# Attention by key with stacked hi and lo operands, and one output product for all mixer blocks

## What is computed

```python
x = x + 0.5 * _swiglu(_rmsnorm(x, g_f1), w_g1, w_u1, w_d1)
h = _rmsnorm(x, g_mix)
u, c_gate, b_gate, q, k, v, f_logit, q_mem = jnp.split(h @ w_in, bounds, axis=-1)
y_conv = b_gate * conv                  # conv over c_gate * u, 3 taps, 256 channels
q = _head_rms(q, gq_fox); k = _head_rms(k, gk_fox)            # 8 heads of 64
cum = jnp.cumsum(jnp.concatenate([past_logf, logf], axis=1), axis=1)
# forgetting attention ("fox"), causal; a decode row sees 128 past keys and its own 32
s = q . k * scale + cum_q - cum_k;  y_fox = softmax(s) @ v
# memory attention, 4 heads, 256 memory keys for the prompt, 256 cached ones for decode
y_mem = softmax(q_mem . mk * scale) @ mv
x = x + concat(y_conv, y_fox, y_mem) @ w_out
x = x + 0.5 * _swiglu(_rmsnorm(x, g_f2), w_g2, w_u2, w_d2);  x = _rmsnorm(x, g_fin)
```

## Time and profile before

| | |
|---|---|
| runs | 2314.63 us median of 3 (2314.17 to 2317.61) |
| the profiled execution | 2306.02 us, its span 2304.2 us |
| TensorE (PE) busy | 2118.3 us, 92% |
| VectorE (DVE) busy | 1183.0 us, 51% |
| ScalarE (ACT) busy | 749.0 us, 33% |
| GpSimd (POOL) busy | 388.5 us, 17% |
| granted TensorE clock, mean | 0.96 of full speed |
| DMA | 205.78 MB, 89 GB/s |

### The profile page before, as it was taken

The page is one execution under the profiler, slowest core; times in us unless marked ns, Lnnn a source line. Parts: engine busy times, 40 slices in busy tenths (PEclk is TensorE's granted clock), DMA queues, the critical chain, the costliest instruction groups (busy, mean ns, idle before and its releaser), DMA issues.

```text
span 2304.2 us, 40450 instructions
## 1 busy us (share of the span) xinstructions
PE 2118.3 (92%) x15785; PEld 2027.2 (88%) x15785; DVE 1183.0 (51%) x2332; ACT 749.0 (33%) x1385; POOL 388.5 (17%) x290
## 2 busy tenths in 40 slices
PE   4599999999999879899999989966999999999996
PEld 4599999999999879779788777765999999999996
DVE  6855566556320063545544556677655665643103
ACT  5332222324221241152433433443232232433213
POOL 0000000004444422221221223100000000143440
PEclk7799999999999989899999998987999999999997
DMA  4512222228532114311020210132222222385222
GB/s 150 140 57 83 84 81 88 70 77 301 175 123 92 46 29 37 62 29 56 23 79 23 55 51 18 44 113 83 77 73 84 84 75 90 116 297 168 89 68 85
DMA packets 206427, 205.78 MB, mean 89 GB/s; under 512 B 15864, under 2 KB 150264, under 8 KB 206016
## 3 DMA queue, kind: packets, MB, share of 16 engines
q1 hardware_dynamic: 206272, 203.59, 29.1%
HBM read 161.87 MB, written 41.69 MB: 88 GB/s over the span
## 4 chain that ended last, share of the span: by engine, by line
PE 52%; DVE 5%; issue 2%; ACT 2%; DMA 1%; another core or an unknown queue 0%; POOL 0%; DVEq 0%; ACTq 0%; SPq 0%
PE banks L256 14%; PE banks L257 14%; PE banks L258 14%; PE banks L1994 3%; PE banks L2033 3%; PE banks L2014 2%; PE banks L1761 1%; PE banks L1945 1%; DVE xT L1563 1%; DVE row_bias L1641 1%; DMA x_again<-x_spill 1%; DVE w_raw L1708 0%; DVE hforms_lo L1415 0%; DVE hforms_f L1399 0%; PE banks L2096 0%
## 5 line engine op out<-in xcount | busy, mean ns | idle before, releaser
L256 PE MATMUL banks<-hforms_hi,w_hi 128*128 128x264 f32 x2112 | 604.2, 286 | 65.7 <-DVE hforms_lo L1415 44.6
L257 PE MATMUL banks<-hforms_lo,w_hi 128*128 128x264 f32 x2112 | 606.2, 287 | 0.0
L258 PE MATMUL banks<-hforms_hi,w_lo 128*128 128x264 f32 x2112 | 603.0, 286 | 0.0
L256 PEld LDWEIGHTS banks<-hforms_hi,w_hi 128*128 128x128 f32 x2112 | 402.3, 190 | 68.9 <-issue 35.8
L747 POOL TENSOR_TENSOR w_lo<-w_raw,w_hi 128x1024 fp32r<-128x1024 f32 x88 | 219.6, 2498 | 1311.8 <-ACT w_hi L992 1311.8
L258 PEld LDWEIGHTS banks<-hforms_hi,w_lo 128*128 128x128 f32 x2112 | 402.1, 190 | 0.0
L257 PEld LDWEIGHTS banks<-hforms_lo,w_hi 128*128 128x128 f32 x2112 | 401.1, 190 | 0.0
L256 PE MATMUL banks<-acts_a,w_hi 128*128 128x264 f32 x896 | 255.3, 285 | 1.8 <-DVE acts_a L1433 1.8
L258 PE MATMUL banks<-acts_a,w_lo 128*128 128x264 f32 x896 | 255.2, 285 | 0.0
L257 PE MATMUL banks<-acts_a,w_hi 128*128 128x264 f32 x896 | 255.1, 285 | 0.0
L992 ACT ACTIVATE w_hi<-w_raw 128x1024 fp32r<-128x1024 f32 x88 | 93.3, 1060 | 347.8 <-PE banks L258 305.4
(11 more groups left out here) (260 smaller groups left out, 4135.7 us busy)
## 6 DMA issues: line engine op xcount, KB each, us to landing
w_raw<-in_w_ffn_down SPq DMA_DIRECT2D x88, 512.0 KB, 4.0
w_raw<-in_w_ffn_gate SPq DMA_DIRECT2D x48, 512.0 KB, 5.2
w_raw<-in_w_ffn_up SPq DMA_DIRECT2D x48, 512.0 KB, 5.2
act_rows<-act_f SPq DMA_DIRECT2D x44, 528.0 KB, 2.8
acts_f<-act_rows SPq DMA_DIRECT2D x44, 528.0 KB, 5.0
w_raw<-in_w_in SPq DMA_DIRECT2D x20, 512.0 KB, 6.1
x_spill<-xT SPq DMA_DIRECT2D x4, 2112.0 KB, 9.3
xT<-x_spill SPq DMA_DIRECT2D x2, 4224.0 KB, 16.6
```

What stands on the lines that cost most here:

```text
L256: eng.matmul(out, w_hi, x_hi, start=first, stop=False, skip_group_check=added)
L257: eng.matmul(out, w_hi, x_lo, start=False, stop=False, skip_group_check=added)
L258: return eng.matmul(out, w_lo, x_hi, start=False, stop=last, skip_group_check=added)
```

## The change

Attention is made by key. K is held as hi twice (`k_hi_twice`, KS1: head j's rows and a copy on the other 64 rows) and as lo with a row of ones (`k_lo_and_one`, KS2); Q as hi over lo (`q_hi_lo`, Q1) and as hi with a row of minus the row's maximum (`q_hi_and_max`, Q2), all in fp32r. One matmul Q1·KS1 gives scores by query, which serve for the maxima only: 18 units, each with VectorE's pass, whose elementwise result is now dropped (L1682). The maxima are turned (L2069, L2070) and copied into Q2 by ScalarE. Then `keyed` makes the scores by key, KS1·Q1 + KS2·Q2 (L2095, L2096), with the maxima already subtracted, for 28 blocks of up to 512 queries (12 in a memory pair); ScalarE takes the exponential with −F as bias by key (L1163), which is the turned form that `weigh` needs (L2109): `v_and_ones` is stationary, up to 512 queries move, and the output has the weighted values on 64 rows and the sum on the other 64. ScalarE makes a rough reciprocal of the sum (L1174, L1176), VectorE finishes it and scales (`mixed`, three instructions). All the maxima of a pair but for the order of their turns stand ahead of its first keyed block.

The mixer's output of a group goes to HBM (`mix_rows`). `xT` is stored at the end of the first SwiGLU, its room is used for the new operands, and it is loaded again. At the end one product over all eight blocks sums in eight PSUM banks, 576 matmuls in 3 chunks of (k = 0 to 3, 4 to 6, 7), with 24 adds instead of 192. The w_out blocks are split by ScalarE and GpSimd, the mixer blocks by ScalarE and VectorE; the first four w_out hi and mix hi lie in the last memory pair's keyed stage. The conv groups have no output product, and the forget gates come after the second. Loops are unrolled.

The core of the diff:

```diff
             def conv_hi(it):
...
-                act.wait_ge(L["oloaded"], 16 * it + 16)
-                if it:
-                    act.wait_ge(L["odone"], 24 * it)
-                else:
-                    act.wait_ge(FFN["down_done"], 4 * NF)
-                act.activation(whi[:, 3, :], raw[:, 3, :], ACT.Copy).then_inc(L["o_hi"], 1)
+                    else:
+                        act.wait_ge(CONVS["proj"], 9 * it)
+                    act.activation(whi[:, b, :], raw[:, b, :], ACT.Copy).then_inc(W["hi"], 1)
...
+                def q_hi(c):
+                    s, w = CHUNKS[c]
+                    act.wait_ge(A["nrm"], nrm0 + nrm_count(kind, c + (3 if kind == "fox" else 0)))
+                    for q in (Q1, Q2):
+                        for j in range(PAIR):
+                            act.activation(q[half_rows(j), j, s:s + w], qT[half_rows(j), s:s + w], ACT.Copy)\
+                                .then_inc(A["qhi"], 1)
...
+                def sum_rough(x):
+                    n, j, b, w, s = PARTS[kind][x]
+                    r = half_rows(1 - j)
+                    act.wait_ge(A["pv"], b0 + n + 1)
...
+                    act.activation(lr[r, 0:w], bank(b, w)[r], ACT.Ln).then_inc(A["rough_sum"], 1)
+                    act.wait_ge(A["rough_sum"], at + 1)
+                    act.activation(lr[r, 0:w], lr[r, 0:w], ACT.Exp, scale=-1.0).then_inc(A["rough_sum"], 1)
...
+                def q_lo(c):
+                    s, w = CHUNKS[c]
+                    for j in range(PAIR):
+                        dve.wait_ge(A["qhi"], 12 * g + 4 * c + j + 1)
+                        r = half_rows(j)
+                        dve.tensor_tensor(Q1[half_rows(1 - j), j, s:s + w], qT[r, s:s + w],
+                                          Q1[r, j, s:s + w].bitcast(F32), ALU.subtract).then_inc(A["qlo"], 1)
...
+                        dve.tensor_tensor_reduce(junk[0:rows, 0:w], PS[0:rows, b:b + w], nF[0:rows, j, k0:k0 + w], 1.0,
+                                                 -3e38, ALU.add, ALU.max, m).then_inc(A["smax"], 1)
...
-            def resid(kind, it):
-                L = LOOPS[kind]
-                for m in range(24):
...
-                    dve.wait_ge(L["odone"], 24 * it + m + 1)
-                    dve.tensor_tensor(xT[:, d, s:s + w], xT[:, d, s:s + w], bank(OBANK[kind] + m % 4, w), ALU.add)\
-                       .then_inc(L["resid"], 1)
...
+                def scores(n):
...
+                    if n == 0:
+                        pe.wait_ge(A["nrm"], nrm0 + NRM[kind])
+                        pe.wait_ge(A["qhi"], 12 * g + 12)
+                        pe.wait_ge(A["qlo"], 6 * g + 6)
+                        pe.wait_ge(A["khi"], 2 * g + 2)
+                        pe.wait_ge(A["kdve"], 4 * g + 2)
...
+                    else:
+                        pe.wait_ge(A["smax"], 18 * g + n - 1)
...
+                def keyed(n):
...
+                    if n >= 2:
+                        pe.wait_ge(A["expd"], b0 + n - 1)
+                    at = 512 * (2 + n % 2)
+                    dst = PS[0:kr, at:at + w]
+                    pe.matmul(dst, KS1[:, j, kc:kc + kr], Q1[:, j, q0:q0 + w], start=True, stop=False)
+                    mm = pe.matmul(dst, KS2[:, j, kc:kc + kr], Q2[:, j, q0:q0 + w], start=False, stop=not diag)
...
+                def weigh(n):
...
+                    pe.wait_ge(A["expd"], b0 + n + 1)
...
+                    pe.matmul(PS[:, 512 * ob + oc:512 * ob + oc + w], VO[0:kr, vo, j, :], PRT[0:kr, (b0 + n) % 4, 0:w],
+                              start=first, stop=last, skip_group_check=True).then_inc(A["pv"], 1)
...
+            for c, (s, w) in enumerate(CHUNKS):
+                for ks in ((0, 1, 2, 3), (4, 5, 6), (7,)):
+                    for d in range(KT):
+                        if ks[0] == 0 and c:
+                            pe.wait_ge(OUT["resid"], KT * (c - 1) + d + 1)
...
+                            mm = split3(pe, bank(OBANK[d], w), h[:, k % 4, ds], l[:, k % 4, ds], hh[:, k, s:s + w],
+                                        hl[:, k, s:s + w], k == 0, k == KT - 1)
```

## The result

The ratio is 1.0182, with a 95% interval of 1.0161 to 1.0203: slower by 42 us, where 12 were forecast, and above the range's upper end of 2348. The profiled executions are 2306.02 and 2356.07 us, 50 apart, because the profiled one of before lies 8 us under its own median.

A forecast was written before the change was run, and what follows sets the result against it. TensorE was taken as the bound (52% of the span). Convolution −28.4, fox pairs −47.0, memory pairs −8.4 and −1.9, output product +92.4, FFN2 +2 sum to +8.7; with the clock +11.7, 2326.2 us, range 2294 to 2348.

The follow-up runs named there:

- E1: Changed kernel with six of the second head's score units (memory pairs: three times two) issued between the first head's key blocks; 2340.6 us, ratio 1.0137.
- E5: Attention by query from the kernel before, with the changed kernel's convolution, forget gates and single output product, first chunk k by k; 2311.0 us, ratio 0.9993.
- E6: Changed kernel with six fox score units under key blocks, GpSimd's weight splitting held, two rough-sum buffers, first output-product chunk k by k; 2319.8 us, ratio 1.0035.

## What to carry to other kernels

When a change takes work out from in front of a stage, list every transfer and store that this work covered, and where each is issued, before counting the gain: here such waits ate a gain of 6 to 10 us, and moving three steps brought 14. Where a new step shares a buffer between two engines, look at what stands behind the wait in the waiting engine's queue. And the cost of an idle TensorE is not only its length: matmuls behind it went at the lower clock, at a price of some 2 us behind 4.9 us of idle, in a stage that had looked as if VectorE alone set its pace.

## What the runs showed of the hardware

- A granted clock of 0.57 to 0.58 in the first 4 us of projections, once after a keyed stage in which TensorE had been busy for 32.04 of 32.9 us, behind two of four fox pairs of the changed kernel and behind none of E1. Behind all four pairs of both kernels the last 2 us in front of the projections are alike (TensorE busy for 1.48 of 2.00, at 1.00). What sets it off was not found.
- VectorE's reciprocal of 64 × 512 values from PSUM took 3355 ns in the mean. The two operations that it replaced on VectorE take 0.69 us each. Of 64 × 32 values it took 354 ns.
- Of two 1 KB stores of strided columns in E5 the second landed 17.9 us after its issue, the first 10.6, and three transfers of 0.5 MB issued right behind them took 20 to 21 us. In E6 a 64 KB load of past keys issued 2.4 us behind the second store, and behind the three large ones, landed after 21.5 us; the same load in E5, issued 50 us later, took 4.9. Which of these transfers held the others no run shows.
